# Asking for the two transfers of the gate buffer on ScalarE's queue instead of SyncE's

## The reference, cut to what matters

```python
PEER_HEADS = 8
PEER_NKEYS = 128
PEER_TOPK = 16
PEER_N_EXPERTS = PEER_NKEYS ** 2
```

## Time and profile before

| | |
|---|---|
| median of 3 runs | 3785.98 us (3782.63 to 3792.16) |
| profiled execution | 3787.69 us, span 3786.4 us |
| TensorE busy | 3567.0 us, 94% of the span |
| VectorE busy | 2188.7 us, 58% |
| ScalarE busy | 1532.1 us, 40% |
| GpSimd busy | 488.5 us, 13% |
| transfers of GST to `gdram` | 24, 1024.0 KB each |

### The profile page before, as it was taken

The page is one execution under the profiler, slowest core; times in us unless marked ns, Lnnn a source line. Parts: engine busy times, 40 slices in busy tenths (PEclk is TensorE's granted clock), DMA queues, the critical chain, the costliest instruction groups (busy, mean ns, idle before and its releaser), DMA issues.

```text
span 3786.4 us, 49772 instructions
## 1 busy us (share of the span) xinstructions
PE 3567.0 (94%) x20631; PEld 3015.2 (80%) x20631; DVE 2188.7 (58%) x3689; ACT 1532.1 (40%) x2278; POOL 488.5 (13%) x421
## 2 busy tenths in 40 slices
PE   7998999999989989999989999999989888999999
PEld 6755778888876567887777788799988888988989
DVE  3275463333374645445555435389898875666666
ACT  3245532212233563223455433333565665333332
POOL 0000000000000000000000101003333343343340
PEclk9999999999999999999999999999999999999999
DMA  6400113333211012222221233258687889888884
GB/s 251 160 1 1 56 56 111 112 123 111 101 45 70 1 45 78 100 93 106 84 82 43 96 112 123 82 176 279 232 279 245 293 298 329 324 318 316 323 325 161
DMA packets 169650, 581.56 MB, mean 154 GB/s; under 512 B 13984, under 2 KB 80656, under 8 KB 131536
## 3 DMA queue, kind: packets, MB, share of 16 engines
q1 hardware_dynamic: 113824, 365.46, 27.7%
q0 software_dynamic: 55600, 212.91, 15.8%
HBM read 516.97 MB, written 61.34 MB: 153 GB/s over the span
## 4 chain that ended last, share of the span: by engine, by line
PE 36%; DVE 7%; DMA 3%; ACT 3%; issue 2%; POOL 0%; SPq 0%; DVEq 0%; ACTq 0%; POOLq 0%
PE ps L667 9%; PE ps L669 9%; PE ps L668 9%; DMA gdram<-GST 2%; PE ps L3230 2%; DVE WL L538 1%; DVE UB L3060 1%; PE ps L2350 1%; PE ps L2369 1%; PE ps L2577 1%; PE ps L2591 1%; ACT GST L2933 1%; PE ps L2897 1%; DVE OH L2960 0%; DVE OH L2964 0%
## 5 line engine op out<-in xcount | busy, mean ns | idle before, releaser
L538 DVE TENSOR_TENSOR WL<-stage,WH 128x2048 fp32r<-128x2048 f32 x239 | 546.4, 2286 | 378.5 <-ACT WH L528 376.5
L667 PE MATMUL ps<-HH,WH 128*128 128x512 f32 (+1 forms) x1672 | 619.7, 371 | 24.0 <-DVE HL L993 16.2
L528 ACT ACTIVATE WH<-stage 128x2048 fp32r<-128x2048 f32 x239 | 455.3, 1905 | 390.9 <-PE ps L669 366.4
L668 PE MATMUL ps<-HL,WH 128*128 128x512 f32 (+1 forms) x1672 | 611.3, 366 | 0.0
L669 PE MATMUL ps<-HH,WL 128*128 128x512 f32 (+1 forms) x1672 | 608.5, 364 | 0.0
L667 PE MATMUL ps<-HP,WH 128*128 128x384 f32 (+1 forms) x1088 | 380.8, 350 | 21.4 <-DVE WL L538 20.2
L667 PEld LDWEIGHTS ps<-HH,WH 128*128 128x128 f32 x1672 | 317.3, 190 | 89.2 <-issue 28.3
L668 PE MATMUL ps<-LP,WH 128*128 128x384 f32 (+1 forms) x1088 | 374.3, 344 | 0.0
L669 PE MATMUL ps<-HP,WL 128*128 128x384 f32 (+1 forms) x1088 | 373.9, 344 | 0.0
L669 PEld LDWEIGHTS ps<-HH,WL 128*128 128x128 f32 x1672 | 316.5, 189 | 53.7
L668 PEld LDWEIGHTS ps<-HL,WH 128*128 128x128 f32 x1672 | 317.3, 190 | 50.7 <-issue 1.2
(11 more groups left out here) (476 smaller groups left out, 5872.6 us busy)
## 6 DMA issues: line engine op xcount, KB each, us to landing
stage<-in_w SPq DMA_DIRECT2D x64, 1024.0 KB
stage<-in_u SPq DMA_DIRECT2D x64, 1024.0 KB
stage<-in_v SPq DMA_DIRECT2D x64, 1024.0 KB
stage<-in_w_mod SPq DMA_DIRECT2D x40, 1024.0 KB
adram<-GA SPq DMA_DIRECT2D x128, 192.0 KB
gdram<-GST SPq DMA_DIRECT2D x24, 1024.0 KB
GR<-gdram POOLq DMA_DIRECT2D x32, 768.0 KB
AR<-adram POOLq DMA_DIRECT2D x32, 768.0 KB
```

The source lines that it names most:

```text
L528: act.e.activation(k.WH[o % 2][:, 0:w], k.stage[n % 2][:, 0:w], ACT.Copy).then_inc(*act.done("slab_hi", n))
L538: dve.e.tensor_tensor(k.WL[o % 2][:, 0:w], k.stage[n % 2][:, 0:w], k.WH[o % 2][:, 0:w].bitcast(F32), ALU.subtract).then_inc(*dve.done("sla ...
L667: pe.e.matmul(o, wh[:, kk, cs], L.view(L.hh, kk, z), start=first, stop=False)
L668: pe.e.matmul(o, wh[:, kk, cs], L.view(L.hl, kk, z), start=False, stop=False)
```

## The change

The two transfers of a full GST leave `sync_route`, which goes away, and are written in `scalar_route` directly behind the eviction of the fourth batch, with a wait of ScalarE for its own eviction. `io` is handed down to `scalar_route`. The rest of the diff takes out the branches that `on_pool` never took; `dot_end(j)` becomes `("dot_v", j)`.

```diff
-def scalar_route(k, act, pieces):
+def scalar_route(k, act, io, pieces):
...
                 act.e.activation(k.GST.of(key)[:, :, o:o + 8].rearrange("p n t -> p t n"),
                                  k.psw.of(("g", tt, b))[:, :].rearrange("p (t n) -> p t n", t=8),
                                  ACT.Copy).then_inc(*act.done("g", (tt, b)))
-        elif kind == "dot" and on_pool(tt):
-            row = k.UB.of(("u", tt))
-            act.wait_ge("dot_mul", tt)
-            act.e.activation(row[:, :], row[:, :], ACT.Copy, accum_out=k.A[:, tt:tt + 1]).then_inc(*act.done("dot_s", tt))
+                if b % 4 == 3:
+                    act.wait_ge("g", (tt, b))
+                    for half, z in (("a", slice(0, 16)), ("b", slice(16, 32))):
+                        act.e.dma_start(io["gdram"][4 * tt + b // 4, z].rearrange("n p c -> p n c"),
+                                        k.GST.of(key)[:, :, :].rearrange("p (n c) t -> p n (c t)", n=32)[:, z]).then_inc(
+                            *act.landed(f"gst_{half}", key))
...
-def sync_route(k, sp, io, pieces):
-    for kind, tt, i in pieces:
-        if kind == "spread" and i >= 2:
-            for b in evicted(i):
-                if b % 4 == 3:
-                    key = (tt, b // 4)
-                    sp.wait_ge("g", (tt, b))
-                    for half, z in (("a", slice(0, 16)), ("b", slice(16, 32))):
-                        sp.e.dma_start(io["gdram"][4 * tt + b // 4, z].rearrange("n p c -> p n c"),
-                                       k.GST.of(key)[:, :, :].rearrange("p (n c) t -> p n (c t)", n=32)[:, z]).then_inc(
-                            *sp.landed(f"gst_{half}", key))
...
             sp.wait_ge("gelu", (g, c))
             sp.e.dma_start(io["adram"][g, :, NDENSE * c:NDENSE * c + NDENSE], k.GA.of((g, c))[:, :]).then_inc(*sp.landed(f"aw{c}", g))
-            sync_route(k, sp, io, next(route, []))
```

More of the change, by code:

```diff
@@ L55 @@
     "route_evicted": ("qp", "keys", "g_exp", "chosen", "gated", "g"),
-    "row_evicted": ("xt", "dot_s", "ag", "wt", "window", "row_out"),
+    "row_evicted": ("xt", "ag", "wt", "window", "row_out"),
     "mix_evicted": ("z_act", "m_hi", "y", "relu", "act_hi", "down0"),
@@ L74 @@
     "row_sums": ("expert", "u_index", "row_gate", "v_index", "dot_v", "wg", "sx_out"),
-    "row_scaled": ("dot_mul", "windows_zeroed"),
+    "row_scaled": ("windows_zeroed",),
     "peer_rows": ("w_mul", "w_lo", "pd", "x_out"),
@@ L2837, in dot_calls @@
     return [max(c, PHASES[0][2] + 2) for c in calls]
[L2840 to L2845, removed]
 def fetch_call(calls, j):
@@ L3055, in vector_route @@
             dve.e.tensor_copy(k.IDXT[:, :], k.psn.of(("chosen", tt))[:, 0:128]).then_inc(*dve.done("v_index", 0))
-        elif kind == "dot" and not on_pool(tt):
+        elif kind == "dot":
             row = k.UB.of(("u", tt))
@@ L3067, in pool_route @@
             pool.wait_ge("u_index", 0)
-            row = k.UB.take(pool, ("u", tt), dot_end(tt))
+            row = k.UB.take(pool, ("u", tt), ("dot_v", tt))
             pool.e.indirect_dma_start(row[:, :], None, io["u_rows"],
@@ L3114, in scalar_gelu, with scalar_early @@
         *act.done("gelu", (g, c)))
-def scalar_early(k, act):
+def scalar_early(k, act, io):
     route = route_order()
@@ L3121, in scalar_early @@
             scalar_gelu(k, act, g, c)
-            scalar_route(k, act, next(route, []))
+            scalar_route(k, act, io, next(route, []))
     act.mark("route")
@@ L3158, in sync_early @@
 def sync_early(k, sp, io):
-    route = route_order()
     base = k.slab_of[("u", 0), 0]
@@ L3244, in scalar_rows_out @@
     if slot == GATED:
-        act.wait_ge(*dot_end(DOTS - 1))
+        act.wait_ge("dot_v", DOTS - 1)
         act.e.activation(k.AG[:, :], k.A[:, :], ACT.Gelu_apprx_tanh).then_inc(*act.done("ag", 0))
@@ L3325, in pool_rows_in @@
         if n == 0:
-            pool.wait_ge(*dot_end(DOTS - 1))
+            pool.wait_ge("dot_v", DOTS - 1)
         if n == 5:
@@ L3383, in tensor_program, with scalar_program @@
     tensor_late(k, pe)
-def scalar_program(k, act):
+def scalar_program(k, act, io):
     scalar_start(k, act)
@@ L3396, in scalar_program @@
     scalar_queries(k, act)
-    scalar_early(k, act)
+    scalar_early(k, act, io)
     scalar_late(k, act)
@@ L3475, in build @@
         tensor_program(k, pe)
-        scalar_program(k, act)
+        scalar_program(k, act, io)
         vector_program(k, dve)
```

## The result

The changed kernel took 3797.97 us (median of 9 runs, 3793.61 to 3800.74) against 3785.3 us (9 runs) for the kernel before: a ratio of 1.0034, 95% interval 1.0024 to 1.0044, so 12.7 us slower. The profiled execution of after has a span of 3796.7 us, 10.3 us more than the one of before.

A forecast was written before the change was run, and what follows sets the result against it. TensorE, busy 94% of the span, was taken as the bound, with VectorE also near full in the routing part. Seven terms summed to +7.6 us on the median 3785.98, giving 3794 us; mechanism bounds -1 to +18 us, range 3770 to 3814.

The forecast's parts named there:

- Term 1: Start of GST's pair: asked for at E, landings earlier by the DMA engines' idle time; -3.1 us, bounds 0 and -15.7.
- The hold: ScalarE held by GST's pair: about 8 us in groups 0, 2, 6; 3 in group 4; some 65 in all.
- rival 2: ScalarE's GST pair gets the engines before SyncE's slab, holds shrink to 3 us; -13 us, 3773 us, chance 0.20.
- Term 2: Groups 0, 2, 6 and 9: most of ScalarE's hold is absorbed; 0 us, bounds 0 and +2 us each.
- Terms 3 and 4: Group 1: hold makes WH late, WL starts 2.1 us late, +2.1 us; groups 3, 5, 7 alike, +2.4 us.
- Term 5: Group 8: one-hot scaling late behind ScalarE's hold, TensorE loses 4.2 us, some 2 given back; +2.2 us.
- Term 6: Group 10: the next slab, no longer held on SyncE, passes GST's packets; +2.5 us (0 to 3.7).
- Term 7: Last group: a slab passes GST's tail and the landing slips; +1.5 us (0 to 3.3).
- The signs named beforehand: Start within 0.1 us of E, second issue 7 to 9 us, GST wait halved, WH wait +10 us, slabs unheld.
- rival 1: Splits: holds of groups 1, 3, 5 and 7 reach TensorE in full; +22.9 us, 3809 us, chance 0.22.

The follow-up runs named there:

- e1: The kernel before with only the dead on_pool branches taken out, SyncE still asking for the pair (the control): ratio 0.9998.
- e2: The kernel before, with SyncE sending the slab behind the GST pair in calls that complete a group: 3769.53 us, ratio 0.9951.
- e3: The changed kernel, with ScalarE asking for half a of GST only and SyncE for half b: ratio 1.0022.
- e5: The changed kernel with gdram laid out so that a transfer is 128 pieces of 8 KB, not 2048 of 512 bytes: ratio 0.9941.
- e7: The changed kernel, but GpSimd asks for both halves of GST, behind its row fetch of the call: ratio 0.9989.
- e9: The changed kernel, with SyncE sending the slab of a group-completing call only once the fourth eviction is done: 3803.65 us, ratio 1.0035.
- e6: The changed kernel, with SyncE sending no further slab after a group-completing call until both halves of GST have landed: ratio 1.0008.
- e10: e3 with SyncE sending no further slab after a group-completing call until both halves of GST have landed: ratio 0.9986.

## Why the prediction came out as it did

The forecast, 3794 us and slightly slower, was 4 us off. The mechanism it named, a hold on ScalarE that reaches TensorE, is there, but shorter than put; several terms were wrong and offset each other, so that the size came out is luck. The range beside the sum, -1 to +18 us, is not that of the terms' own bounds, which add up to -11.4 to +25.6 us; the 12.7 us lie within both. The table has E (end of the fourth eviction) of both kernels, what each group adds to the lateness of the next E (for the last, of the end), what the terms had put there, and the same step of other kernels.

| group | E before | E after | after | terms | e1 | e2 | e3 | e5 | e7 | e9 |
|---|---|---|---|---|---|---|---|---|---|---|
| 0 | 2734.75 | 2736.64 | -3.1 | -0.2 | +1.5 | -2.9 | -1.6 | -2.8 | -3.1 | -1.6 |
| 1 | 2775.17 | 2773.99 | +4.3 | +2.1 | +1.1 | +1.2 | +4.4 | +1.2 | +4.4 | +4.4 |
| 2 | 2808.12 | 2811.24 | +1.8 | -0.3 | +0.8 | -7.6 | -2.2 | -7.6 | -4.2 | +0.9 |
| 3 | 2843.93 | 2848.88 | +2.2 | +0.8 | +0.1 | +2.5 | -0.1 | +2.5 | +3.2 | +4.0 |
| 4 | 2903.58 | 2910.78 | -2.9 | -2.5 | +2.7 | -2.9 | +0.2 | -2.9 | -4.2 | -2.8 |
| 5 | 2943.81 | 2948.14 | +3.1 | +0.8 | -1.0 | +3.1 | -0.1 | +3.1 | +2.9 | +3.1 |
| 6 | 2978.10 | 2985.54 | +1.6 | -0.1 | 0 | -7.4 | -3.9 | -7.4 | -5.4 | +1.6 |
| 7 | 3013.17 | 3022.20 | +0.6 | +0.8 | -0.6 | +0.1 | +0.2 | +0.1 | +0.6 | +2.2 |
| 8 | 3060.18 | 3069.80 | +3.7 | +2.2 | 0 | -0.5 | +4.1 | +3.0 | +4.8 | +7.1 |
| 9 | 3090.84 | 3104.18 | -7.7 | 0 | -0.3 | -7.3 | -3.7 | -8.2 | -7.5 | -1.3 |
| 10 | 3129.67 | 3135.32 | +5.7 | +2.5 | -1.6 | -0.8 | +7.8 | -2.8 | +3.0 | +7.2 |
| 11 | 3156.16 | 3167.46 | -1.0 | +1.5 | | | | | | |

After sums to +8.4, the terms to +7.6. The control shows that equal kernels scatter by up to 2.7 us in a step.

**The start (Term 1).** Group 4 gave what was put there and group 0 more, but the way to the number failed. "The engines were full anyway" counted bytes and left out whose bytes go first: e2 moves the same bytes, asks for the pair ahead of one slab, and gains 17 us, more than the bound of 15.7. The step that failed is pricing a start by the idle time of the DMA engines.

**The hold.** Put at 7 to 9 us for the second request in groups 0, 2 and 6, 3 us in group 4, some 65 us in all. Groups 2 and 6 have 7.5 and 6.6 us, groups 0 and 4 both 1.9, and the 24 issues take 49 us. In groups 0 and 4 the slab was asked for some microseconds after the pair, and waited itself: in group 0 it was asked for at 2739.59 and moved from 2744 on, 4.4 us later, where the DMA shares of before had given 1.4. That is half of rival 2 (and of its sign: a second request of 1.9 us in group 0, but the slab's own request was not held), whose counter-argument was that nothing in the trace of before showed one queue holding up another; a trace in which only one queue asks in this way can't show it. The other half of rival 2 fails: once it moves, the slab passes GST by turns of packets, as the earlier trace rows had it. The Trainium skill, "Perfetto Trace Analysis", section "DMA Instruction — HWDGE (DVE, Sync)", says that the generator of descriptors is locked for one user and that an issue contains the wait for it. This trace agrees only by half: SyncE's slab does wait, but its request takes its usual 0.33 us, and beside ScalarE's 7.91 us in group 2 SyncE's adram request took 0.67 us.

**Absorbed holds (Term 2).** In groups 2 and 6 it held nearly: +1.8 and +1.6 us. The table shows what was forgone there: kernels in which the landing is early gain 7.5 us in each (e2, e5). Group 9 was put at 0 and gained 7.7: ScalarE waited 2.4 us before the eviction (8.9 in before), which came 16.3 us behind E, not 23.2. It is no chance of phase, since e2, e5 and e7 gain as much there. It goes with the slab no longer standing just ahead of the pair (3101.87 us is 2.3 us ahead of E, 3089.33 was 1.5) or with fewer rows fetched beside it (4 requests from 2 us before E to 16 us behind it, 7 before). e3 speaks for the rows: its slab stands 3.1 us ahead, it fetches 7 rows, and it gains only 3.7 us. Settled it isn't.

**Terms 3 and 4.** Groups 1, 3, 5 and 7 cost 4.3 + 2.2 + 3.1 + 0.6 = 10.2 us where 4.5 had been put, but not for the reason given. e2, in which ScalarE asks for nothing, has nearly the same, +2.5, -2.9 and +3.1, in groups 3 to 5, and e3 and e7, without a hold, have +4.4 in group 1. These steps come back in kernels that share only a changed start of the groups; what makes them is open. The hold's own part is seen in two places: in TensorE's wait for WL, 29.5 to 30.1 us in the three kernels with long holds (after, e6, e9) and 21.7 to 27.9 in the seven others that change anything, so, as an estimate, some 5 of the 11.0 us; and in e6 against e10, 8 to 10 us, of which the groups' steps have 6.0 in group 8 (+6.5 and +0.5).

**Group 8 (Term 5).** +3.7 us, put at 2.2, and +7.1 in e9. The second request was held 5.88 us, as foreseen. But e7 has +4.8 and e3 +4.1 without a hold, from landings waited for 6.7 and 5.9 us, so either suffices.

**What the move lets through (Term 6).** Right and under-sized: two slabs went by in group 10, not one. SyncE, then the chain of after:

```profile
3143.40 0.33 SPq L494 DMA_DIRECT2D stage<-in_u  x1
...
3151.31 0.33 SPq L494 DMA_DIRECT2D stage<-in_v  x1
```
```profile
3135.75 13.37 DMA gdram<-GST
...
3150.87 6.08 issue
...
3167.89 8.73 DMA gdram<-GST
...
3178.26 10.49 DMA AR<-adram
```

Neither slab is held (4.88 us in the earlier trace rows), the landing comes 21.6 us behind E where it was 14.7, and ScalarE waits 6.08 us instead of 0.5; the group adds 5.7 us. e3 and e9, with slabs as free, have +7.8 and +7.2 there; e2, where they stay behind the pair in one queue, -0.8. The tail (Term 7) cost nothing: 8.73 us to the landing, 9.10 in the earlier trace rows, and 10.49 us of reading back, 11.14 there.

**The signs named beforehand.** Right: the start at E; no slab request held on SyncE (0.33 us each). Half right: the second request, 7.5 and 6.6 us in groups 2 and 6, but 1.9 in group 0. Wrong: ScalarE's wait before GST fell by a quarter (38.3 to 28.1), not by half; VectorE's wait for WH fell (49.7 to 45.8) where 10 us more were predicted, since the lateness shows one engine further on, as TensorE's wait for WL. That wait stayed under the 40 us named for rival 1. So the size came out right by luck: costs put too low (groups 1, 3, 5, 8 and 10) met a gain of 7.7 us in group 9 that no term had.

## What to carry to other kernels

Before moving a transfer to an idle engine's queue, look at its issue: one of 2048 pieces is 0.37 us alone and up to 9 us behind another, and whatever stands behind it in that engine's program pays. SyncE, which only asks for transfers, could bear that here; ScalarE couldn't. Price a landing by what is ahead of it in its own queue and by the packet size of what shares the engines with it, not by idle engines; and where an order matters, keep both transfers in one queue, or check in the trace that the second really starts behind the first. If a spill is written in 512-byte pieces, widen them first: that was worth 22 us, while changing the queue alone cost 13. And look at the single requests before a timeline's merged row is called a hold: SyncE's 8.32 us in group 2 are one request of 0.67 us, a wait for a gelu, and one of 0.32 us.

## What the hardware showed that I had not expected

- A transfer asked for by SyncE can wait for ScalarE's without any sign in its request: a slab asked for 2.9 us after ScalarE's pair first moved 4.4 us later, while its request took 0.33 us.
- Requests of the same 2048 pieces take a constant 1.2 us on GpSimd (1199 to 1232 ns, 24 times) and 0.37 to 7.5 us on ScalarE.
- Two queues share by packet whatever the size: 180 packets of 8 KB went beside 182 of 512 bytes in 5 us, 1.00 MB of a slab to 0.09 MB of GST.
- Eight-kilobyte pieces bring the longest request from 9.1 us to 0.7 us in the same place.
